# A fused MoE layer on one Trainium2 core: down result scaled once in float32, scattered by float32 matmuls

## The reference

```
top_w = g_w * top_p / jnp.sum(top_p, axis=-1, keepdims=True)
combine = sum(one_hot(expert_id, N_EXPERTS) * top_w[..., None], axis=-2)
hid = silu(einsum('bsd,edf->bsef', h, w_gate)) * einsum('bsd,edf->bsef', h, w_up)
hid = hid * combine[..., None]
y   = einsum('bsef,efd->bsd', hid, w_down)
x   = layer_norm(ALPHA * x + g2 * y)
```

## Time and profile before

| | us |
|---|---|
| median of three runs | 1087.92 |
| the profiled execution | 1086.85 |
| its span, first to last instruction | 1085.1 |
| PE busy in it | 967.4 |
| DVE busy | 326.5 |
| ACT busy | 230.6 |

### The profile page before, as it was taken

The page is one execution under the profiler, slowest core; times in us unless marked ns, Lnnn a source line. Parts: engine busy times, 40 slices in busy tenths (PEclk is TensorE's granted clock), DMA queues, the critical chain, the costliest instruction groups (busy, mean ns, idle before and its releaser), DMA issues.

```text
span 1085.1 us, 15639 instructions
## 1 busy us (share of the span) xinstructions
PE 967.4 (89%) x6820; PEld 590.2 (54%) x6820; DVE 326.5 (30%) x744; ACT 230.6 (21%) x475; POOL 39.6 (4%) x60
## 2 busy tenths in 40 slices
PE   3999899998899898978879998999998989897875
PEld 1887758777743333334248876687884333332421
DVE  2112323222851312111170132331276231211215
ACT  2102314200251312111121132241014231211211
POOL 1100000010000000000010000000001000000000
PEclk9899999999999999998989999999999999999998
DMA  9938854586439999999875426766442999999970
GB/s 381 409 141 348 335 224 155 219 318 274 160 132 422 389 427 429 429 427 423 374 304 219 161 63 239 316 272 209 182 174 82 413 428 429 429 430 429 422 310 39
DMA packets 38526, 324.60 MB, mean 299 GB/s; under 512 B 4920, under 2 KB 5048, under 8 KB 9392
## 3 DMA queue, kind: packets, MB, share of 16 engines
q1 hardware_dynamic: 33696, 308.82, 69.6%
q0 software_dynamic: 4320, 13.28, 3.5%
q10 hardware_dynamic: 432, 1.39, 0.3%
HBM read 321.05 MB, written 2.42 MB: 298 GB/s over the span
## 4 chain that ended last, share of the span: by engine, by line
PE 75%; DMA 10%; DVE 6%; ACT 5%; issue 3%; SPq 1%; DVEq 0%; ACTq 0%
PE ps L768 13%; PE ps L666 9%; PE ps L817 8%; PE ps L692 6%; PE ps L872 5%; PE ps L944 5%; PE ps L958 5%; PE ps L781 5%; DMA expert_gate_up<-in_w_gu 4%; DMA expert_down<-in_w_dn 3%; PE ps L595 3%; PE ps L725 2%; PE ps L616 2%; DMA dense<-in_w_ada 2%; PE ps L827 2%
## 5 line engine op out<-in xcount | busy, mean ns | idle before, releaser
L768 PE MATMUL ps<-expert_gate_up,gathered_prompt 128*32 128x512 f32 x768 | 172.4, 603 | 5.0 <-ACT gathered_sample L1143 2.3
L768 PE MATMUL ps<-expert_gate_up,gathered_sample 128*32 128x512 f32 x768 | 172.4, 603 | 0.0
L817 PE MATMUL ps<-expert_down,hiddenT 128*32 128x512 f32 x1024 | 117.5, 602 | 11.8 <-ACT gathered_sample L1143 4.5
L666 PE MATMUL ps<-hT,dense 128*128 128x256 f32 x512 | 115.9, 385 | 0.0
L768 PEld LDWEIGHTS ps<-expert_gate_up,gathered_prompt 128*32 128x32 f32 x768 | 49.8, 111 | 115.6 <-issue 112.9
L666 PEld LDWEIGHTS ps<-hT,dense 128*128 128x128 f32 x512 | 97.4, 192 | 16.1 <-issue 2.8
L1557 DVE SCALAR_TENSOR_TENSOR y_lo<-ps,slot_weight,y_hi 128x512 fp32r<-128x512 f32 x64 | 48.1, 751 | 105.7 <-ACT y_hi L1175 105.6
L817 PEld LDWEIGHTS ps<-expert_down,hiddenT 128*32 128x32 f32 x1024 | 32.0, 110 | 82.8 <-issue 57.4
L1540 DVE TENSOR_TENSOR hidden<-hidden,ps 128x256 f32<-128x256 f32 x32 | 13.4, 420 | 194.0 <-ACT hidden L1159 194.0
L692 PE MATMUL ps<-dense,hT 128*128 128x256 f32 (+1 forms) x320 | 69.3, 381 | 1.7 <-ACT hT L1100 1.7
L692 PEld LDWEIGHTS ps<-dense,hT 128*128 128x128 f32 x320 | 60.6, 201 | 10.4 <-ACT hT L1100 2.5
(11 more groups left out here) (217 smaller groups left out, 1110.1 us busy)
## 6 DMA issues: line engine op xcount, KB each, us to landing
expert_gate_up<-in_w_gu SPq DMA_DIRECT2D x64, 2048.0 KB, 17.6
expert_down<-in_w_dn SPq DMA_DIRECT2D x64, 1024.0 KB, 12.9
dense<-in_w_ada SPq DMA_DIRECT2D x48, 1024.0 KB, 9.1
dense<-in_w_in SPq DMA_DIRECT2D x28, 1024.0 KB, 9.3
dense<-in_w_o SPq DMA_DIRECT2D x8, 1024.0 KB, 6.3
dense<-in_w_out SPq DMA_DIRECT2D x8, 1024.0 KB, 5.1
dense<-in_w_c SPq DMA_DIRECT2D x4, 1024.0 KB, 24.6
gate<-ada_rows POOLq DMA_DIRECT2D x4, 1024.0 KB, 8.5
```

The lines of the kernel that those rows point to most:

```text
L666: last = mm(b[:, m * 256:(m + 1) * 256], w[:, k, m * P:(m + 1) * P], hT[:, k, :], start=(k == 0), stop=(k == KD - 1))
L768: last = mm(ps[r0:r0 + 32, q, :], xg[s][:, k, at_:at_ + CAP], w_gu[(i * EPI + 2 * q + j) % SLOTS][:, k, :], start=(k == 0), stop=(k == KD ...
L817: last = mm(ps[32 * e:32 * e + 32, banks[c], :], h, w_dn[(i * EPI + e) % SLOTS][:, f, c * 512:(c + 1) * 512], start=(f == 0), stop=(f == 1 ...
```

## The change

The split is dropped. `y` is one float32 tile. For each request ACT scales half 0 out of bank 2 and DVE half 1 out of bank 3, each waiting only for its own half of `down` and for the weights. The scatter is one float32 matmul of 512 columns for each half, and `selT` is float32. The next `down` waits for `y0_done` (bank 2) or `y1_done` (bank 3). In the last iteration DVE used to run `low` of half 0 ahead of the norm's `scale` of request 0 and `low` of half 1 behind it; now there is one scaling, behind it.

```diff
-        y_hi = arena("y_hi", 52, [P, 2, D], F32R)
-        y_lo = arena("y_lo", 60, [P, 2, D], F32R)
+        y = arena("y_weighted", 52, [P, 2, D])
-        selT = arena("selectT", 68, [P, 2, 2, P], F32R)
+        selT = arena("selectT", 68, [P, 2, 2, P])
...
                 for c in range(2):
                     if paired and s:
-                        pe.wait_ge(*reached(w, "lo_done", 4 * g + c + 1))
+                        pe.wait_ge(*reached(w, ("y0_done", "y1_done")[c], 2 * g + 1))
...
             def scatter(w, g, i, s, first):
                 for c in range(2):
-                    pe.wait_ge(*reached(w, "lo_done", 4 * g + 2 * s + c + 1))
-                    for hp, part in enumerate((y_hi, y_lo)):
-                        last = mm(ps[:, 4 + 2 * s + c, :], selT[:, i % 2, s, :], part[:, s, c * 512:(c + 1) * 512],
-                                  start=(first and hp == 0), stop=True, skip_group_check=True)
+                    pe.wait_ge(*reached(w, ("y0_done", "y1_done")[c], 2 * g + s + 1))
+                    last = mm(ps[:, 4 + 2 * s + c, :], selT[:, i % 2, s, :], y[:, s, c * 512:(c + 1) * 512],
+                              start=first, stop=True, skip_group_check=True)
...
-            def high(w, g, i, s, c, bank, copies):
+            def weighted(w, g, i, s, bank, copies):
                 act.wait_ge(*reached(w, "selT_copied", copies))
-                act.wait_ge(*reached(w, "y_filled", 4 * g + 2 * s + c + 1))
-                actf(y_hi[:, s, c * 512:(c + 1) * 512], ps[:, bank, :], ACT.Copy,
-                     scale=wsl[:, i % 2, s:s + 1]).then_inc(w["hi_done"], 1)
+                act.wait_ge(*reached(w, "y_filled", 4 * g + 2 * s + 1))
+                actf(y[:, s, 0:512], ps[:, bank, :], ACT.Copy, scale=wsl[:, i % 2, s:s + 1]).then_inc(w["y0_done"], 1)
...
-            def low(w, g, i, s, c, bank):
-                dve.wait_ge(*reached(w, "hi_done", 4 * g + 2 * s + c + 1))
-                at_ = slice(c * 512, (c + 1) * 512)
-                V.scalar_tensor_tensor(y_lo[:, s, at_], ps[:, bank, :], wsl[:, i % 2, s:s + 1],
-                                       y_hi[:, s, at_].bitcast(F32), ALU.mult, ALU.subtract).then_inc(w["lo_done"], 1)
+            def weighted(w, g, i, s, bank, copies):
+                dve.wait_ge(*reached(w, "selT_copied", copies))
+                dve.wait_ge(*reached(w, "y_filled", 4 * g + 2 * s + 2))
+                V.tensor_scalar(y[:, s, 512:1024], ps[:, bank, :], wsl[:, i % 2, s:s + 1], None,
+                                ALU.mult).then_inc(w["y1_done"], 1)
```

More of the change, by code:

```diff
@@ L303, in build @@
         NAMES = ("sel_ready", "xg_filled", "xg_act", "xg_dve", "selT_filled", "selT_copied", "h_filled", "silu_done",
-                 "hid_done", "hidT_filled", "hidT_copied", "y_filled", "hi_done", "lo_done", "sc_filled")
+                 "hid_done", "hidT_filled", "hidT_copied", "y_filled", "y0_done", "y1_done", "sc_filled")
         PER_LAYER = {"sel_ready": 2 + PAIRS - 1, "xg_filled": KD * (PAIRS + 1), "xg_act": 4 * (PAIRS + 1),
@@ L308, in build @@
                      "hidT_filled": ITERS + 2, "hidT_copied": ITERS + 2, "y_filled": 4 * ITERS,
-                     "hi_done": 4 * ITERS, "lo_done": 4 * ITERS, "sc_filled": 2 * ITERS}
+                     "y0_done": 2 * ITERS, "y1_done": 2 * ITERS, "sc_filled": 2 * ITERS}
         main = {n: sem(n) for n in PER_LAYER}
@@ L1062, in _ @@
                 turn_request(m, i, 1, 1)
-                pe.wait_ge(*reached(m, "lo_done", 4 * i + 2))
+                pe.wait_ge(*reached(m, "y0_done", 2 * i + 1))
+                pe.wait_ge(*reached(m, "y1_done", 2 * i + 1))
                 down(m, None, i, i, 1, (2, 3), False, ITERS + 2)
@@ L1188, in extra_round @@
                         for s in range(2):
-                            for c in range(2):
-                                high(w, g, i, s, c, 2 + c, g + 1)
+                            weighted(w, g, i, s, 2, g + 1)
             act.dma_start(cond_in[:, :, :], io["cond"]).then_inc(start_in, 16)
@@ L1271, in _ @@
                 silu(m, 0, 1, 0)
-                for c in range(2):
-                    high(m, 0, 0, 0, c, EARLY_BANK[c], 1)
+                weighted(m, 0, 0, 0, EARLY_BANK[0], 1)
                 turned_request(m, 1, 0, 2)
-                for c in range(2):
-                    high(m, 0, 0, 1, c, 2 + c, 2)
+                weighted(m, 0, 0, 1, 2, 2)
                 for i in range(1, ITERS - 1):
@@ L1285, in _ @@
                     for s in range(2):
-                        for c in range(2):
-                            high(m, i, i, s, c, 2 + c, i + 2)
+                        weighted(m, i, i, s, 2, i + 2)
                     if i + 1 == SPLIT_AT:
@@ L1298, in _ @@
                 turned_request(m, 0, 0, ITERS + 1)
-                for c in range(2):
-                    high(m, i, i, 0, c, 2 + c, i + 2)
+                weighted(m, i, i, 0, 2, i + 2)
                 silu(m, i, 1, 1)
@@ L1303, in _ @@
                 sqrt(8, 9)
-                for c in range(2):
-                    high(m, i, i, 1, c, 2 + c, i + 2)
+                weighted(m, i, i, 1, 2, i + 2)
                 if l + 1 < DEPTH:
@@ L1573, in extra_round @@
                         for s in range(2):
-                            for c in range(2):
-                                low(w, g, i, s, c, 2 + c)
+                            weighted(w, g, i, s, 3, g + 1)
                 dve.wait_ge(*reached(w, "sc_filled", r * (2 * ITERS) + 2 * ITERS))
@@ L1748, in _ @@
                 hidden_product(m, 0, 1, 0)
-                for c in range(2):
-                    low(m, 0, 0, 0, c, EARLY_BANK[c])
+                weighted(m, 0, 0, 0, EARLY_BANK[1], 1)
                 select_T(m, 0, 1, (1,), 2)
-                for c in range(2):
-                    low(m, 0, 0, 1, c, 2 + c)
+                weighted(m, 0, 0, 1, 3, 2)
                 select(m, 1, (0, 1), pos)
@@ L1767, in _ @@
                     for s in range(2):
-                        for c in range(2):
-                            low(m, i, i, s, c, 2 + c)
+                        weighted(m, i, i, s, 3, i + 2)
                     if i == 2:
@@ L1786, in _ @@
                 hidden_product(m, i, 0, 0)
-                for c in range(2):
-                    low(m, i, i, 0, c, 2 + c)
+                weighted(m, i, i, 0, 3, i + 2)
                 moe_sum(l, 0)
@@ L1793, in _ @@
                 centre(y_sum, ln2, 0)
-                low(m, i, i, 1, 0, 2)
                 scale(e, ln2, 0, 8, x2_ready, l)
-                low(m, i, i, 1, 1, 3)
+                weighted(m, i, i, 1, 3, i + 2)
                 more = l + 1 < DEPTH
```

## The result

| | before | after |
|---|---|---|
| median | 1087.61 us (14 runs) | 1093.28 us (14 runs, 1089.38 to 1101.7) |
| ratio, 95% interval | 1 | 1.0065 [1.0043, 1.0087] |
| profiled execution | 1086.85 us | 1091.75 us |
| its span | 1085.1 us | 1090.0 us |
| PE, DVE, ACT busy | 967.4, 326.5, 230.6 us | 983.4, 302.6, 209.0 us |

The change makes the kernel slower by 0.65%, some 5.7 us in the medians and 4.9 us in the two profiled executions. VectorE and ScalarE lost 24 and 22 us of work, TensorE gained 16. I predicted 1091.2 us, in a range from 1088 to 1096.

A forecast was written before the change was run, and what follows sets the result against it. Expert parts were taken as a race of PE against weight transfers. Layer 0's +1.8 and layer 1's +1.5 us gave +3.3: 1090.2 against the profiled 1086.85, 1091.2 us as median (1.07 above that execution), range 1088.0 to 1096.0.

The forecast's parts named there:

- The scatter, +0.80: Each scatter goes from 1.13 to 1.92 us: four records at 0.43 plus 0.20 for entering and leaving.
- Rival 3: Faster: a float32 pass costs no more than the float32r pair, so scatters add nothing; about -4, 1084 us; chance 0.09.
- The evacuation: Time given back: 0.15 us a down, 0.75 before layer 0's iteration 1, 0.8 at the jump, 1.3 and 0.9 at layer ends.
- rival 2: Queue runs dry, PE decides: PE's count is read only after its matmuls; +8.4, 1096.3 us; chance 0.20.
- Layer 0, +1.8: Layer 0's sum: 2.2 at gate/up load 31, 1.6 and 0.8 for later scatters, -1.3 end, -1.5 clock.
- The jump makes it +4.5: Layer 0: PE's lateness of +5.3 us falls to +4.5 behind the jump after iteration 5, so gu 29 is issued at 509.4.
- Rival 1: PE regains its loss in the race, clock staying up after the wait before iteration 1; within 2.2 us, 1089.5; chance 0.27.
- My own sign: Layer 0: if gu 29 is issued before 507 instead of near 509.4, the slowdown halves.
- I expect it to stay at 2.4 GHz, and take -1.5: Layer 0: PE idles only 0.6 to 1 us before gu 31, so its clock stays up for the pass behind: -1.5 us.
- The load behind a dry queue: Layer 0: gu 29 alone needs 2.3 us before data flows, then 4.9 for 2048 KB, landing at 516.6.
- Layer 1, +1.5: PE 4.3 us late at gu 29 but no queue gap, so gu 31 unchanged; then +1.6, +0.8, -0.9.
- The range's lower end: 1088.0 us: the sum with 0.59 for a scatter (16 that count, some -2.5) and one more clock fall gone.

The follow-up runs named there:

- scatter-alone kernel: Kernel before with only the scatter changed, one float32 matmul of y_hi per half, old evacuation and waits kept: 1097.83 us, 1.0101 of before.
- the order alone: Changed kernel with DVE's scaling of the last half put ahead of the norm's scale again in the last iteration: 1096.8 us, 1.0088 of before.
- the kernel with 16: Changed kernel with 16 never-executed transposes added in the body of PE's extra rounds: 1091.2 us, 1.0037 of before.
- with 40: Changed kernel with 40 never-executed transposes added in the body of PE's extra rounds: 1091.62 us, 1.0038 of before.
- padded kernel before: Kernel before with the same 40 never-executed transposes: 1087.53 us, 1.0001 of before.
- the evacuation alone: Changed kernel with two float32r scatter matmuls per half again, both on the same rounded tile, low part left out: 1083.69 us, 0.9967 of before.
- rounded single scatter: Changed kernel with one float32r scatter matmul per half, low part left out: 1080.61 us, 0.9943 of before.
- doubled kernel: Changed kernel with halved slot weights and every float32 scatter matmul done twice: 1135.2 us, 1.0434 of before.

## Why the prediction was right, and where not

**What bounds the kernel** (a race of PE against the transfers, decided at gu 29): right. The margins and the rising price of a scatter show it.

**The scatter, +0.80**: 1.13 to 1.91, +0.78, and 2.04 to 3.63 for a pair. Of the projection's 0.43 a record every digit held. Rival 3 fell with it. Before the first of a scatter's weights the loader was idle for 0.84 us; that it was a column group that stood idle, as I wrote, no row shows, and the 0.20 doesn't rest on it.

**The evacuation**: `down` -0.14 for -0.15; the wait before iteration 1 -0.71 for -0.75; the jump, from the end of `down` to the restart, -0.75 for -0.8 in layer 0 and -0.38 in layer 1 (the scatter-alone kernel shows that PE's sequencer runs ahead, which sinks rival 2's mechanism); the end of layer 0 -1.14 for -1.3, and the order alone is worth 1.5; the end of layer 1, from the start of the last `down` to the end of the last scatter, -0.82 for -0.9. The experiment puts all of it at -3.2 us.

**Layer 0, +1.8**: about +0.65 (+1.79 to the last scatter, -1.14 behind it). Two steps failed and covered each other.
- *"The jump makes it +4.5"* failed: gu 29 was issued only 0.1 us later. The PE time was added, and the clock gave it back: the pass of iteration 1 ran at 2.4 GHz (-1.7), and so did the first of iteration 6, 13.97 us for 15.67 with the pass behind it (-1.7); from the restart to that pass the mean granted clock was 0.74 where it had been 0.64, -0.5. That is 3.9 of the 4.4 us. Rival 1 named the first of these; I had given it 0.27. My own sign had come too: counted from the gather as before, the issue is at 505.0, ahead of the 507 below which I expected half the slowdown.
- *"I expect it to stay at 2.4 GHz, and take -1.5"* failed: PE stood 2.17 us before gu 31 (2.90 before), since it wasn't late, and the pass behind took 8.77 us again, for 8.55 before.
- What came behind held: +1.59 for two scatters, +0.78 for the third, -1.14 for the end.
- The load behind a dry queue was undersized: from issue to landing 8.3 us where I took 7.2 (2.3 and 4.9).

Stretches from the restart behind the jump to the first pass of iteration 6, layer 0 and layer 1 (columns as above), first before:

```profile
485.30:496.10 10.80, 8.80 (x39) 7.53 (x41) 4.58 (x13) 4.08 (x8) 0.61 (x1) 0.64 1.00 420
1004.00:1013.90 9.90, 7.29 (x38) 6.38 (x39) 4.57 (x13) 4.08 (x8) 0.80 (x2) 0.77 1.00 417
```

and after:

```profile
484.60:494.90 10.30, 8.18 (x38) 6.80 (x39) 4.57 (x13) 4.08 (x8) 0.60 (x1) 0.74 1.02 431
1005.40:1020.80 15.40, 8.98 (x40) 8.05 (x41) 4.58 (x13) 4.08 (x8) 0.84 (x2) 0.56 0.89 375
```

**Layer 1, +1.5**: 8.0, the step that failed. I had PE 4.3 us late at gu 29, 0.5 us before the queue would run dry, and so "gu 31 lands where it did". It was 10.0 us late. The hole takes 4.2 of them (198.2 against 194.0 with 16 more instructions), the rest is my 4.3 and 1.5 more. Of these 1.5 the kernel with 16 spends 1.3 between the restart and the first pass, at a mean granted clock of 0.55 where before had 0.77 (the second row of each pair above; the changed kernel has 0.56). The cover of 4.8 us was used up, and 6.1 us arrived at gu 31. With the hole away the layer ends 245.9 us after its gather with 16 and 249.3 with 40. The padded kernel before has 244.3 and the unpadded one 242.2, so what is left of the loss is between +1.6, which is my term, and +7.1. One profile of each doesn't settle how much of this layer's loss is the change's own.

**The sum, +3.3**: 5.7 measured, 3.7 and 4.1 where the code lies elsewhere. By layers the profile of after says +0.65 and +8.0 for my 1.8 and 1.5. Its total is only +4.9 because this execution came to the gather of layer 0 3.0 us earlier and was 0.8 us quicker in layer 1's dense part, neither of which the change touches. So this profile came near my sum by luck: the two expert parts together lost 8.7 us, and 3.8 us of the dense parts took most of the miss back. The miss is the 6.5 us in layer 1, part of which is an effect of placement that I didn't know. By the medians the sum was 2.4 us short, within the range. The range's lower end doesn't follow from its own terms: 16 x (0.80 - 0.59) is 3.4 us, not 2.5, and with a clock fall of 1.7 the sum would end at 1086.1, not 1088; the result doesn't touch it. What stays open: the share of layer 1's loss that is the change's own, and what makes the changed kernel's executions spread.

**Which version to take.** The gain sits in the evacuation, the loss in the number format of the scatter: the evacuation alone is 3.2 us faster than before and the float32 scatter 11.0 us slower. The rounded single scatter is the fastest at 1080.61 us, 0.9943 [0.9926, 0.9959], for one who can do without the low part.

## What to carry to other kernels

Price a PE edit in a stretch where transfers and PE race by the margin of the next load (last landing less its issue), not by a share of its busy time: the same microsecond cost roughly 0.2, 0.4 and 0.8 here. Read idle stretches for what they do to the clock behind them too, since a wait that goes can give back more than its length (0.71 us and 1.7 behind it here). And before a small difference is explained by what was changed, shift the code behind the nearest jump by some dead instructions and time it again, and look for instruction transfers in the idle stretch.

## What the runs showed of the hardware that I had not expected

- A hole of 4.7 to 4.9 us in PE's instruction stream, a few matmuls behind a taken jump, at one place in three kernels; 16 instructions that are never executed remove it. It ends 2.3 to 2.4 us behind the start of a 16 KB instruction packet.
- The jump itself leaves PE idle for 3.9 to 7.2 us in nine kernels, and matmuls queued ahead of it run under that time: 3.6 us of them cost nothing, and in the doubled kernel, with 7.1 us of them, the restart comes only 0.2 us later and PE is idle for 1.3 and 0.8 us.
- A 2048 KB load that finds the queue empty landed after 8.3 and 8.5 us in the changed kernel, and after 7.7 to 9.8 in all profiles; gu 30 lands 4.85 us behind gu 29 in layer 0.
- The 0.71 us shorter wait before iteration 1 made the pass behind it 1.7 us shorter, at 2.4 GHz instead of part of it at 1.2.
- DVE's plain scaling of 128x512 out of PSUM takes 751 ns, as long as the scale and subtract with a second input that it replaces (0.75).
